# Expert rows: empty slots skipped by bounds, results scattered in token order

## The chip, the cores and the metric

The kernel runs on one core of a Trainium2 chip. The metric is the device time of one execution in microseconds (us).

## The reference, cut to what matters

The program is two transformer blocks. The second one has, in each of its two layers, a mixture of experts over T tokens of width D = 1024 (T = 512 in the first layer, 256 in the second): a router picks 2 of 32 experts per token, each expert is a gated feed-forward net of width 512, and a token's two results are added with their gates.

```python
def hier_moe(xf, ...):
    ...
    top_v, top_i = lax.top_k(e_in, TOP_K)
    gate = jax.nn.softmax(top_v, axis=-1) * g_val
    expert = g_idx * EXPERTS_PER_GROUP + top_i
    ...
    def expert_block(args):
        xblk, e = args
        return (jax.nn.silu(xblk @ w1[e]) * (xblk @ w3[e])) @ w2[e]
    yb = lax.map(expert_block, (xb, block_exp)).reshape(R, D)
    out = jnp.zeros((T + 1, D), yb.dtype).at[row_tok].add(yb * row_gate[:, None])
    return out[:T]
```

Everything is in float32. An expert's three matrices are 6.29 MB, so the 32 experts of a layer are 201 MB.

## The kernel before, in words

The stages run in order: four feed-forward nets with two mixers between them (first block), then `even`, `moe(0)`, `odd`, `moe(1)` (second block). Only `moe` and its router are touched by the change.

The router (VectorE, `moe` from line 1871) gives each of a token's two assignments a slot. A block is 64 slots (`BLK`) of one expert; block b belongs to expert b, and an expert's slots fill from the first. Extra blocks (16 and 8) exist for experts with more than 64 tokens; they are walked only if there are any. TensorE turns one-hot matrices into the table `token_of_slot` (line 918), where an empty slot gets token 0, and VectorE copies it out (line 1993). `slot_of_token` (line 1959) holds the slot of each assignment.

The expert loop handles one block per step, on all engines at once:

- SP (lines 550 to 582) loads the expert's weights in six pieces of 1 MB, four for w1 and w3 (named raw and work in the trace, both <-in_w) and two for w2, into six buffers. A load waits until TensorE has used the buffer (`expert_done`).
- GpSimd (`gather`, `rows_of`, lines 2172 to 2182) copies the block's column of the table, drains, and issues an indirect DMA that fetches all 64 rows of 4 KB from `router_rows` into `xg`, which has two buffers. It waits until TensorE has turned the rows that were in the buffer (`xgt_ready`), two blocks back.
- TensorE (`block_of`) does w1 and w3 for block b (lines 934, 936), turns the rows of b + 1 (line 927), does w2 for b - 1 (line 952) and turns the result of w1 and w3 (line 944).
- ACT copies the turned rows and the products, computes tanh, and stores the result of block b - 1 with two plain DMAs of 128 KB (line 1413) into `expert_rows`, ordered by slot.
- VectorE computes the activation and copies w2's result from PSUM to `ysb` (line 2015, `y_copied`), which has two buffers: it waits for the store two blocks back (`y_stored`).

After the loop GpSimd waits for all stores and gathers each token's two rows from `expert_rows` with indirect DMAs (line 2203), two per tile of 128 tokens: eight in the first layer, four in the second, 0.5 MB each. Before it waits for them, ACT in the first layer issues loads of the next layer's norm rows and makes the high halves of two weight panels (line 1128; VectorE's low halves are line 1537). It then scales the first row by its gate (line 1459), and VectorE adds the second row, multiplies, and adds to the residual (lines 2050 to 2054).

Once, early in the program (line 1316), ACT issues a 4 MB DMA that fills the rows of the extra blocks in `expert_rows`.

## Time and profile before

| | |
|---|---|
| median of 3 runs | 2908.72 us (2908.54 to 2909.84) |
| the profiled execution | 2905.86 us |
| its span, first to last instruction | 2904.0 us |
| TensorE busy (PE) | 2310.4 us, 80% |
| VectorE busy (DVE) | 1070.7 us, 37% |
| ScalarE busy (ACT) | 686.9 us, 24% |
| GpSimd busy (POOL) | 117.8 us, 4% |
| mean granted TensorE clock | 0.90 |
| data moved by DMA | 718.82 MB, mean 248 GB/s |

The profile is one execution. Its times count from the first instruction. PE is TensorE's matmuls, PEld its weight loads, SP the engine that issues the weight DMAs; a name that ends in q (SPq, ACTq, POOLq) is an engine's queue of instructions that issue or wait. The DMA share is the mean busy share of the core's 16 DMA engines; it can read a little over 1, where packets overlap. "Idle before" an instruction is the time its engine did nothing, with what ended it. The first expert stage runs from about 1484 to 2046 us, the second from about 2338 to 2892 us.

### The profile page before, as it was taken

To read this page: it belongs to the slowest core of one execution; us is meant where nothing else is said; L and a number is where in the kernel's file an instruction comes from. 1 tells how busy PE (TensorE), PEld (TensorE's weight loads), DVE (VectorE), ACT (ScalarE), POOL (GpSimd) and SP (SyncE) were. 2 spreads that over 40 slices of the span, in tenths; PEclk is the share of its full clock that TensorE was granted. 3 is DMA by queue.
4 is the path that set the end of the run, shared out by engine and by line. 5 is a ranking of instruction groups with operands and counts; after the bars stand their busy time and mean duration, and the time that the engine had idled before them with its cause. 6 is when DMAs were issued, how large, how long until landed. Compare 5 with 4: busy or idle time off the path is not lost.

```text
span 2904.0 us, 35200 instructions
## 1 busy us (share of the span) xinstructions
PE 2310.4 (80%) x13750; PEld 1590.7 (55%) x13750; DVE 1070.7 (37%) x1570; ACT 686.9 (24%) x876; POOL 117.8 (4%) x209
## 2 busy tenths in 40 slices
PE   5998679979987699699558777877369668888885
PEld 5888478878885688587523333332355523333332
DVE  4555545555556355723420100010668410000011
ACT  3334433333335233321101000100335200000100
POOL 0001000000010000000000000000100000000000
PEclk9999789989998799899669999999679788998898
DMA  7775137757752287422149999999420269999997
GB/s 260 261 238 173 56 118 266 253 190 266 262 169 88 104 288 259 139 78 94 73 161 401 399 396 400 402 400 404 179 71 1 87 258 397 401 399 401 401 402 303
DMA packets 242628, 718.82 MB, mean 248 GB/s; under 512 B 17040, under 2 KB 156560, under 8 KB 189072
## 3 DMA queue, kind: packets, MB, share of 16 engines
q1 hardware_dynamic: 213584, 642.82, 59.7%
q10 hardware_dynamic: 19952, 48.45, 4.6%
q0 software_dynamic: 8976, 25.90, 3.0%
q8 instruction: 87, 1.43, 0.2%
q14 instruction: 29, 0.24, 0.0%
HBM read 693.70 MB, written 25.26 MB: 248 GB/s over the span
## 4 chain that ended last, share of the span: by engine, by line
PE 55%; DMA 26%; DVE 9%; issue 4%; DVEq 2%; ACT 2%; SPq 1%; ACTq 0%; POOL 0%; POOLq 0%
DMA raw<-in_w 24%; PE ps L620 13%; PE ps L621 12%; PE ps L622 12%; PE ps L934 10%; PE ps L655 2%; PE ps L634 1%; SPq L554 1%; PE ps L936 1%; PE ps L1071 1%; DVE t_lo L1537 1%; PE ps L1086 1%; DMA raw<-in_ffn_w_up 1%; DVE work L1601 1%; DMA work<-expert_rows,slot_of_token 1%
## 5 line engine op out<-in xcount | busy, mean ns | idle before, releaser
L1537 DVE TENSOR_TENSOR w_lo<-raw,w_hi 128x2048 fp32r<-128x2048 f32 x180 | 411.4, 2290 | 445.1 <-ACT w_hi L1128 445.1
L620 PE MATMUL ps<-t_hi,w_hi 128*128 128x256 f32 (+1 forms) x1568 | 456.4, 291 | 8.7 <-DVE t_lo L1537 8.6
L621 PE MATMUL ps<-t_lo,w_hi 128*128 128x256 f32 (+1 forms) x1568 | 454.1, 290 | 0.0
L622 PE MATMUL ps<-t_hi,w_lo 128*128 128x256 f32 (+1 forms) x1568 | 451.1, 288 | 0.0
L1128 ACT CAST w_hi<-raw 128x2048 fp32r<-128x2048 f32 x180 | 342.1, 1903 | 447.5 <-PE ps L622 428.5
L934 PE MATMUL ps<-raw,work 128*64 128x512 f32 x528 | 308.8, 742 | 167.0 <-DMA raw<-in_w 165.6
L2015 DVE COPY work<-ps 128x512 f32<-128x512 f32 x64 | 44.3, 692 | 932.6 <-PE ps L952 932.6
L620 PE MATMUL ps<-w_hi,t_hi 128*128 128x256 f32 (+1 forms) x1088 | 349.8, 322 | 15.3 <-DVE t_lo L1537 12.4
L622 PE MATMUL ps<-w_hi,t_lo 128*128 128x256 f32 (+1 forms) x1088 | 351.1, 323 | 0.0
L621 PE MATMUL ps<-w_lo,t_hi 128*128 128x256 f32 (+1 forms) x1088 | 351.0, 323 | 0.0
L620 PEld LDWEIGHTS ps<-t_hi,w_hi 128*128 128x128 f32 x1568 | 296.6, 189 | 30.4 <-issue 13.2
L936 PE MATMUL ps<-raw,work 128*64 128x512 f32 x528 | 310.5, 745 | 0.0
L622 PEld LDWEIGHTS ps<-t_hi,w_lo 128*128 128x128 f32 x1568 | 297.6, 190 | 4.6
L621 PEld LDWEIGHTS ps<-t_lo,w_hi 128*128 128x128 f32 x1568 | 296.1, 189 | 5.6
L934 PEld LDWEIGHTS ps<-raw,work 128*64 128x64 f32 x528 | 82.7, 167 | 371.0 <-issue 369.2
L934 PE MATMUL ps<-work 128*64 128x512 f32 x496 | 228.9, 605 | 31.9 <-DMA work<-in_w 31.9
L936 PE MATMUL ps<-work 128*64 128x512 f32 x496 | 229.4, 606 | 0.0
L620 PEld LDWEIGHTS ps<-w_hi,t_hi 128*128 128x128 f32 x1088 | 211.2, 194 | 31.7 <-DVE t_lo L1537 13.5
L952 PE MATMUL ps<-raw,work 128*64 128x512 f32 x992 | 226.7, 598 | 0.2 <-DMA raw<-in_w 0.2
L622 PEld LDWEIGHTS ps<-w_hi,t_lo 128*128 128x128 f32 x1088 | 209.5, 193 | 14.1
L621 PEld LDWEIGHTS ps<-w_lo,t_hi 128*128 128x128 f32 x1088 | 209.3, 192 | 13.5
L1394 ACT COPY work<-ps 128x512 f32<-128x512 f32 x64 | 37.5, 586 | 712.2 <-PE ps L936 712.2
(280 smaller groups left out, 2159.1 us busy)
## 6 DMA issues: line engine op xcount, KB each, us to landing
raw<-in_w SPq DMA_DIRECT2D x256, 1024.0 KB, 11.3
work<-in_w SPq DMA_DIRECT2D x128, 1024.0 KB, 10.7
work<-in_w_mod SPq DMA_DIRECT2D x32, 1536.0 KB, 6.5
raw<-in_ffn_w_gate SPq DMA_DIRECT2D x44, 1024.0 KB, 8.8
raw<-in_ffn_w_up SPq DMA_DIRECT2D x44, 1024.0 KB, 10.3
raw<-in_ffn_w_down SPq DMA_DIRECT2D x44, 1024.0 KB, 4.9
raw<-in_w_in SPq DMA_DIRECT2D x18, 1024.0 KB, 5.5
expert_rows<-work ACTq DMA_DIRECT2D x128, 128.0 KB, 7.2
```

Of the source, the lines that this page charges most:

```text
L554: sp.dma_start(expert_raw(m, x).rearrange("p (a n) -> p a n", a=1), src).then_inc(expert_landed[x], 16)
L620: pe.matmul(dst, a[0], b[0], start=start, stop=False)
L621: pe.matmul(dst, a[0], b[1], start=False, stop=False)
L622: return pe.matmul(dst, a[1], b[0], start=False, stop=stop)
L655: mm = pe.matmul(ps[32 * q:32 * q + 32, bank + a // BANK, 0:n], cond[:, kk, :], mod_raw[:, q * MOD_Q + a:q * MOD_Q + a + n], start=True, s ...
L934: first = pe.matmul(ps[0:BLK, 2 + par, :], xT[:, par, kk * BLK:(kk + 1) * BLK], w1[:, j * BANK:(j + 1) * BANK], start=kk == 0, stop=kk == ...
L936: mm = pe.matmul(ps[BLK:P, 2 + par, :], xT[:, par, kk * BLK:(kk + 1) * BLK], w3[:, j * BANK:(j + 1) * BANK], start=kk == 0, stop=kk == KD - 1)
L952: mm = pe.matmul(ps[BLK * half:BLK * half + BLK, 6 + par, :], am[:, par, c * BLK:(c + 1) * BLK], w2[:, j * D + half * BANK:j * D + (half + ...
L1128: act.copy(slot(j)[0], src).then_inc(w_hi_ready, 1)
L1394: act.copy(gusb[:, par, :], ps[:, 2 + par, :]).then_inc(gu_ready, 1)
L1537: return dve.tensor_tensor(dst, src, hi.bitcast(F32), ALU.subtract)
L2015: dve.tensor_copy(ysb[:, par, :], ps[:, 6 + par, :]).then_inc(y_copied, 1)
```

## The change

Three things. The table's entries now hold an assignment instead of a token: 4 * token + 2 * k + half for the row in the result, and that number shifted right by two for the token; an empty slot gets a number beyond every valid one. The gather and the new scatter name a bound, and rows beyond it are skipped. The result goes to `expert_rows` in token order by an indirect DMA from GpSimd (128 rows of 2 KB, two per slot, valid ones only), in place of ACT's two plain stores; a token's two results then lie side by side, and ACT loads them with one plain 1 MB DMA per tile of 128 tokens.

GpSimd's order in the loop is: gather of block b + 4, scatter of block b. The gather waits as before; the scatter waits for VectorE's copy of block b and for the landing of the scatter before it. ACT, after its loop, waits for all scatters, issues the loads, and only then the loads of norm rows and the two weight splits. The fill of the extra rows is dropped. TensorE makes the table for both halves (twice the small matmuls), and the count of extra blocks gets a place per layer.

```diff
-    put("tokid", i[:, None] + P * np.arange(4)[None, :])
+    put("tokid", 2 * (i[:, None] + P * (np.arange(8) % 4)[None, :]) + (np.arange(8) // 4)[None, :] - 4096)
+    put("halfid", 8192 + (i >= BLK))
...
-    y_dram = nc.dram_tensor("expert_rows", (BLOCKS[0] * BLK, D), F32, kind="Internal").ap()
+    y_dram = nc.dram_tensor("expert_rows", (4 * P * 4, BANK), F32, kind="Internal").ap()
...
                 for i in range(2 * nt):
-                    mm = pe.matmul(ps[0:BLK, 2, 0:nb], r_onehot[:, i, :], r_blk[:, i, 0:nb], start=i == 0, stop=i == 2 * nt - 1)
+                    for half in range(2):
+                        mm = pe.matmul(ps[BLK * half:BLK * half + BLK, 2, 0:nb], r_onehot[:, i, :], r_blk[:, i, 0:nb],
+                                       start=i == 0, stop=i == 2 * nt - 1)
...
-                if l == 1:
-                    act.dma_start(y_dram[EXPERTS * BLK:, :], A["w_out"][0][0:EXTRA[0] * BLK, :]).then_inc(extra_filled, 16)
...
-                def store(b, par):
-                    act.wait_ge(y_copied, b0 + b + 1)
-                    for dst, src in out_rows(b * BLK, par):
-                        act.dma_start(dst, src).then_inc(y_stored[par], 16)
...
+                act.wait_ge(expert_done, MAIN * (m + 1))
+                for par in range(2):
+                    act.wait_ge(y_stored[par], 8 * (b0 + EXPERTS))
+                for t in range(nt):
+                    act.dma_start(yg[t].rearrange("p c n -> p (c n)"),
+                                  y_dram.rearrange("(r c) n -> r (c n)", c=4)[t * P:(t + 1) * P, :]).then_inc(yg_landed[t], 16)
                 if m == 0:
-                    act.wait_ge(expert_done, MAIN)
                     act.wait_ge(mod_stored, 64 * 4)
                     norm_rows(10)
                     split(G0["odd"])
                     split(G0["odd"] + 1)
                 for t in range(nt):
-                    act.wait_ge(yg_landed[t], 32 * (m + 1))
+                    act.wait_ge(yg_landed[t], 16 * (m + 1))
...
-                    dve.tensor_copy(slot_id[:, 0:nt, kk], r_sl[:, kk, 0:nt])
...
-                dve.tensor_copy(table[0:BLK, 0:nb], ps[0:BLK, 2, 0:nb])
+                dve.tensor_scalar(rows_table[:, 0:nb], ps[:, 2, 0:nb], 2.0, k("halfid"), ALU.mult, ALU.add)
+                dve.drain()
+                dve.tensor_scalar(table[0:BLK, 0:nb], rows_table[0:BLK, 0:nb], 2, None, ALU.logical_shift_right)
                 dve.drain().then_inc(table_ready, 1)
...
-                        dve.wait_ge(y_stored[par], 16 * (b0 + b - par))
+                        dve.wait_ge(y_stored[par], 8 * (b0 + b - par))
...
-                def rows_of(b, par):
+                def rows_in(b, par):
 
                     pool.tensor_copy(table_col[0:BLK, par:par + 1], table[0:BLK, bass.ds(b, 1)])
                     pool.drain()
                     return pool.indirect_dma_start(out=xg[0:BLK, par, :], out_offset=None, in_=h_dram,
-                                                   in_offset=bass.IndirectOffsetOnAxis(ap=table_col[0:BLK, par:par + 1], axis=0))
+                                                   in_offset=bass.IndirectOffsetOnAxis(ap=table_col[0:BLK, par:par + 1], axis=0),
+                                                   bounds_check=nt * P - 1, oob_is_err=False)
+
+                def rows_out(b, par):
+
+                    pool.tensor_copy(rows_col[:, par:par + 1], rows_table[:, bass.ds(b, 1)])
+                    pool.drain()
+                    return pool.indirect_dma_start(out=y_dram, in_=ysb[:, par, :], in_offset=None,
+                                                   out_offset=bass.IndirectOffsetOnAxis(ap=rows_col[:, par:par + 1], axis=0),
+                                                   bounds_check=4 * nt * P - 1, oob_is_err=False)
...
+                def scatter(b, par, first=False):
+                    pool.wait_ge(y_copied, b0 + b + 1)
+                    if not first:
+                        pool.wait_ge(y_stored[1 - par], 8 * (b0 + b + par))
+                    rows_out(b, par).then_inc(y_stored[par], 16)
...
-                with pool.Fori(1, EXPERTS // 2) as i:
+                gather(2, 0)
+                gather(3, 1)
+                gather(4, 0)
+                scatter(0, 0, first=m == 0)
+                gather(5, 1)
+                scatter(1, 1)
+                with pool.Fori(3, EXPERTS // 2) as i:
                     gather(2 * i, 0)
+                    scatter(2 * i - 4, 0)
                     gather(2 * i + 1, 1)
+                    scatter(2 * i - 3, 1)
+                for b in range(EXPERTS - 4, EXPERTS):
+                    scatter(b, b % 2)
...
-                for par in range(2):
-                    pool.wait_ge(y_stored[par], 16 * (b0 + EXPERTS))
-                for t in range(nt):
-                    for kk in range(2):
-                        pool.indirect_dma_start(out=yg[t][:, kk, :], out_offset=None, in_=y_dram,
-                                                in_offset=bass.IndirectOffsetOnAxis(ap=slot_id[:, t, kk:kk + 1], axis=0)
-                                                ).then_inc(yg_landed[t], 16)
```

## Rows read from the trace of the kernel before

**Rows 1.** Stretches: length, each engine's busy us (instructions), granted clock, DMA share, GB/s

```profile
1850.00:2000.00 150.00, 116.27 (x538) 46.00 (x537) 13.81 (x27) 14.00 (x27) 8.71 (x16) 0.97 1.02 403
...
2500.00:2700.00 200.00, 167.16 (x714) 63.50 (x710) 18.42 (x36) 18.67 (x36) 13.12 (x24) 0.91 1.01 401
```

**Rows 2.** DMA queues and issues, 2400 to 2740 us, with us to landing

```profile
q1 hardware_dynamic: 17211, 125.32, 92.2%
q0 software_dynamic: 1600, 5.24, 5.2%
q10 hardware_dynamic: 3200, 5.25, 4.1%
...
expert_rows<-work ACTq DMA_DIRECT2D x40, 128.0 KB, 7.6
work<-router_rows,token_of_slot_col POOLq DMA_INDIRECT x20, 7.7
```

**Rows 3.** The chain that ended last: start us, us, what

```profile
1560.66 12.93 DMA raw<-in_w
...
1987.40 11.14 DMA raw<-in_w
...
2502.52 10.74 DMA raw<-in_w
2519.39 10.91 DMA raw<-in_w
...
2825.49 10.82 DMA raw<-in_w
```

**Rows 4.** Waits, 2400 to 2840 us, the TensorE line: us, times, longest

```profile
PE ps L934 <- DMA raw<-in_w: 73.2, 26, 3.6
```

**Rows 5.** Busy time by stretch inside two blocks, columns as rows 1

```profile
2502.00:2508.00 6.00, 6.00 (x34) 2.72 (x35) 1.10 (x2) 1.47 (x3) 1.10 (x2) 1.00 1.01 418
2508.00:2511.00 3.00, 2.73 (x14) 0.70 (x10) 0.44 (x2) 0.00 (x0) 0.00 (x0) 1.00 1.02 325
...
2512.00:2519.00 7.00, 5.60 (x19) 2.09 (x20) 0.00 (x0) 0.21 (x1) 0.00 (x0) 0.76 1.02 425
...
2525.00:2528.00 3.00, 2.62 (x14) 0.59 (x10) 0.40 (x1) 0.00 (x0) 0.00 (x0) 1.00 1.04 306
```

**Rows 6.** GpSimd in order of time: start us, us, what, idle before

```profile
2337.93 0.93 POOL L2176 DMA_INDIRECT work<-router_rows,token_of_slot_col  x1 [1.43 <-issue]
2338.86 0.19 POOL L2174 COPY token_of_slot_col<-token_of_slot 64x1 uint32<-64x1 uint32 x1
2342.26 0.92 POOL L2176 DMA_INDIRECT work<-router_rows,token_of_slot_col  x1 [3.20 <-issue]
...
2504.07 0.92 POOL L2176 DMA_INDIRECT work<-router_rows,token_of_slot_col  x1 [0.84 <-issue]
```

**Rows 7.** The chain at the first gather of the second stage

```profile
2337.93 3.55 DMA work<-router_rows,token_of_slot_col
```

**Rows 8.** The final gathers, line 2203: what each took, and DMA to landing

```profile
L2203 POOL DMA_INDIRECT work<-expert_rows,slot_of_token x12: 937/940/2062, 2034.9 to 2888.7; - x12
...
DMA to landing us min/median/max: 4.3/9.3/10.9
```

**Rows 9.** The chain at the end of each expert stage

```profile
2028.30 5.81 DMA expert_rows<-work
...
2036.18 9.96 DMA work<-expert_rows,slot_of_token
...
2881.84 2.38 DMA expert_rows<-work
...
2886.24 5.50 DMA work<-expert_rows,slot_of_token
```

**Rows 10.** The slot tables in order of time, TensorE and VectorE

```profile
1473.21 1.94 PE L918 MATMUL ps<-work 128*64 128x48 f32 x16 [11.44 <-DVEq L1976]
...
1477.05 0.18 DVE L1993 CAST token_of_slot<-ps 64x48 uint32<-64x48 f32 x1
```

More of the change, by code:

```diff
@@ L165, in build @@
         table_col = sb("token_of_slot_col", [P, 2], U32)
+        rows_table = sb("row_of_slot", [P, BLOCKS[0]], U32)
+        rows_col = sb("row_of_slot_col", [P, 2], U32)
         extra_id = sb("extra_expert", [P, EXTRA[0]], I32)
@@ L1403, in tanh, with block_of @@
                                    scale=0.5).then_inc(mtanh_ready, 1)
-                def out_rows(row0, par):
-                    return [(y_dram[bass.ds(row0, BLK), half * BANK:(half + 1) * BANK], ysb[BLK * half:BLK * half + BLK, par, :])
-                            for half in range(2)]
-                def store(b, par):
-                    act.wait_ge(y_copied, b0 + b + 1)
-                    for dst, src in out_rows(b * BLK, par):
-                        act.dma_start(dst, src).then_inc(y_stored[par], 16)
-                def block_of(b, par, last=False, stored=True):
+                def block_of(b, par, last=False):
                     up_copy(b, par)
@@ L1419, in block_of @@
                     tanh(b, par)
-                    if stored:
-                        store(b - 1, 1 - par)
                 rows_T(0, 0)
-                block_of(0, 0, stored=False)
+                block_of(0, 0)
                 block_of(1, 1)
@@ L1430, in moe @@
                 block_of(EXPERTS - 1, 1, last=True)
-                store(EXPERTS - 1, 1)
-                act.wait_ge(extra_filled, 16)
-                used = act.value_load(extra_used[0:1, 0:1], min_val=0, max_val=EXTRA[m])
+                used = act.value_load(extra_used[0:1, m:m + 1], min_val=0, max_val=EXTRA[m])
                 with act.If(used > 0):
@@ L1443, in moe @@
                                        scale=0.5).then_inc(ex_tanh[m], 1)
-                        act.wait_ge(ex_y[m], i + 1)
-                        for dst, src in out_rows((i + EXPERTS) * BLK, 0):
-                            act.dma_start(dst, src).then_inc(ex_stored[m], 16)
+                    act.wait_ge(ex_stored[m], 16 * EXTRA[m])
                     act.drain()
@@ L2028, in moe @@
                 out_rows(EXPERTS - 1, 1, MAIN)
-                used = dve.value_load(extra_used[0:1, 0:1], min_val=0, max_val=EXTRA[m])
+                used = dve.value_load(extra_used[0:1, m:m + 1], min_val=0, max_val=EXTRA[m])
                 with dve.If(used > 0):
-                    dve.wait_ge(y_stored[0], 16 * (b0 + EXPERTS))
+                    dve.wait_ge(y_stored[0], 8 * (b0 + EXPERTS))
                     with dve.Fori(0, EXTRA[m]) as i:
@@ L2037, in moe @@
                         dve.tensor_copy(ysb[:, 0, :], ps[:, 6, :]).then_inc(ex_y[m], 1)
-                        dve.wait_ge(ex_stored[m], 32 * i + 32)
+                        dve.wait_ge(ex_stored[m], 16 * i + 16)
                     dve.drain()
@@ L2181, in gather @@
                         pool.wait_ge(xgt_ready, b0 + b - 1)
-                    rows_of(b, par).then_inc(xg_landed[m][par], 16)
+                    rows_in(b, par).then_inc(xg_landed[m][par], 16)
+                def scatter(b, par, first=False):
[3 more added lines that the diff above has]
+                    rows_out(b, par).then_inc(y_stored[par], 16)
                 gather(0, 0, True)
                 gather(1, 1, True)
-                with pool.Fori(1, EXPERTS // 2) as i:
+                gather(2, 0)
[5 more added lines that the diff above has]
+                with pool.Fori(3, EXPERTS // 2) as i:
                     gather(2 * i, 0)
+                    scatter(2 * i - 4, 0)
                     gather(2 * i + 1, 1)
-                used = pool.value_load(extra_used[0:1, 0:1], min_val=0, max_val=EXTRA[m])
+                    scatter(2 * i - 3, 1)
+                for b in range(EXPERTS - 4, EXPERTS):
+                    scatter(b, b % 2)
+                used = pool.value_load(extra_used[0:1, m:m + 1], min_val=0, max_val=EXTRA[m])
                 with pool.If(used > 0):
                     pool.wait_ge(xgt_ready, b0 + EXPERTS)
+                    for par in range(2):
+                        pool.wait_ge(y_stored[par], 8 * (b0 + EXPERTS))
                     with pool.Fori(0, EXTRA[m]) as i:
-                        rows_of(i + EXPERTS, 0).then_inc(ex_gathered[m], 16)
-                        pool.wait_ge(ex_stored[m], 32 * i + 32)
+                        rows_in(i + EXPERTS, 0).then_inc(ex_gathered[m], 16)
+                        pool.wait_ge(ex_y[m], i + 1)
+                        rows_out(i + EXPERTS, 0).then_inc(ex_stored[m], 16)
+                        pool.wait_ge(ex_stored[m], 16 * i + 16)
                     pool.drain()
```

10 lines of the change are left out of this document (4 added, 6 removed).

## The prediction

> **What bounds the kernel now.** I went from the whole to the part: the busy time by stretch, the DMA queues, the chain of waits, the waits of the engines, and last the stretches inside one block and GpSimd in order of time. Both expert stages run at a DMA share of 1.01 to 1.02 and about 400 GB/s while TensorE is busy 78% and 84% of the time [rows 1]: the reader is to see that the DMA engines, not TensorE, have no room. The queues say what they carry: of 20 blocks' traffic 125.32 MB is weights, 5.24 MB gathered rows, 5.25 MB stored rows [rows 2]. The chain repeats one pattern per expert block: a 10.8 us weight load, TensorE, the next load. Its first and last starts give the period: (1987.40 - 1560.66) / 25 = 17.07 us in the first stage and (2825.49 - 2502.52) / 19 = 17.00 us in the second [rows 3]. Bytes give the same: 6 loads of 1.049 MB are 6.29 MB, gather and store are 0.262 MB each (64 rows of 4 KB), together 6.82 MB, at 401 GB/s 17.0 us. TensorE waits 73.2 us for weights in 26 blocks, 2.8 us per block [rows 4], so a block can shrink to about 14.2 us before TensorE sets its length.
>
> Inside a block the rate is not even. It is 418 to 425 GB/s for most of it, but 325 and 306 GB/s in the 3 us that begin 4 us after a gather is issued [rows 5, 6], at a full DMA share. The gather costs more than its bytes: it drags the weights that move beside it. The stores fall in the stretch at 425 GB/s and do not.
>
> **The parts, priced.** A block has 64 slots, but the two experts of 512 (256) tokens fill only 1024 (512) of the 2048 slots that 32 blocks have. So on average 32 of 64 rows are real in the first stage and 16 of 64 in the second. Before, all 64 are moved.
>
> Gather, price of a full one. From above: its bytes at 425 GB/s, 0.62 us, and the rate lost beside it, 3 x (425 - 325) / 425 = 0.70 us or 3 x (425 - 306) / 425 = 0.84 us [rows 5]; 1.4 us. From below: bytes alone at 401 GB/s, 0.65 us.
>
> Store, price of a full one: 0.62 to 0.65 us by its bytes. The new scatter goes through GpSimd's queue, which the trace has only as gathers, so its price is open: as cheap per byte as a store, or as dear as a gather (1.4 us when full).
>
> First stage, half the rows. Most: 0.70 (gather) + 0.31 (scatter priced as a store) = 1.01 us saved. Least: 0.33 + 0.31 = 0.64 by bytes alone; a dear scatter with a dear gather gives 0.70 - 0.08 = 0.62. Second stage, a quarter. Most: 1.05 + 0.47 = 1.52 us. Least: 0.49 + 0.49 = 0.98 by bytes. I take 0.75 and 1.15 us, nearer to the least, since that needs no more than that bytes not moved take no time, and skipped rows may leave something behind. Over 31 periods each (the first block overlaps the router): 23 + 36 = 59 us; ends 50 and 78 us. The new periods, 16.3 and 15.85 us, stay above TensorE's 14.2 us, so nothing else is late next.
>
> A rule bears on what draws the rate down. The Trainium skill, SBUF — State Buffer, section "SBUF: two separate sides", says DMA reaches SBUF through AXI ports with a swizzled partition map, where DMA engines can contend. By it a gather into 64 partitions crowds half the ports, and a scatter read from all 128 is cheap; the trace agrees as far as 325 GB/s in the gather and 425 in the store go, and by this rule the sum would lie at the upper end, 78 us.
>
> ACT loses two store issues per block and gains four loads per stage: nothing, it waits for TensorE anyway. SP's queue is not touched.
>
> GpSimd gets the scatter, and here queueing matters. An indirect DMA that follows another goes out only after the first has landed: the copy for the second gather is done at 2339.05, yet its DMA goes at 2342.26, 0.8 us after the first one's landing at 2341.48 (2337.93 + 3.55) [rows 6, 7]; with nothing outstanding the gap is 0.84 us. I read that as the drain between copy and DMA. So gather, 0.8 us, scatter, 0.8 us, next gather run in series, and the wait for the previous scatter costs nothing more. A full gather lands in 7.7 us under load, a store in 7.6 us [rows 2]; full size, the series is 16.9 us, just what a block has. With fewer rows the part in which packets move (3 us) halves or quarters: 6.2 + 6.1 + 1.6 = 13.9 us in the first stage, 5.5 + 5.4 + 1.6 = 12.5 us in the second, against 16.3 and 15.85. It stays hidden by 2 to 3 us. Gathers are issued two blocks before TensorE turns them, as before, so latency alone does no harm.
>
> Tables: 16 (8) more small matmuls cost up to 1.9 us, of which some 1.7 us lie beside VectorE's work that ends with the table at 1477.05 [rows 10]; VectorE's extra instruction and drain about 0.3 us, two casts fewer give 0.15 back. Cost 0.3 us per stage. The 4 MB fill of the table's tail goes; nothing waited for it: 0.
>
> Tails. Last rows: the store's landing (5.81 and 2.38 us) [rows 9] gives way to copy, drain, scatter: about 1 us before it and a gather's idle-queue landing of 3.55 us [rows 7], so 2 us later. In its place four (two) plain 1 MB loads from ACT replace pairs of gathers that took 9.96 and 5.50 us to land after their second issue [rows 9], about 2 us better, as GpSimd's 1.0 us start and the 0.5 MB pieces go. Together 0, bounds 3 us either way per stage. In the first stage the last scatter also waits for the one before it, and ACT's two weight splits now stand behind its wait for the scatters; both lie beside the landing. If that cover is gone they cost up to the 3 us.
>
> Sum: -59 + 0.6 + 0 = -58 us. The profiled execution took 2905.86 us (span 2904.0), which gives 2848; the median of the runs is 2.9 us above it, so 2851 us.
>
> **Rivals.**
> (a) Uneven shedding. Real rows fill the first slots. If each DMA engine serves fixed rows, those with the first rows shed little, and a 1 MB load lands when its slowest share does. If the busiest keeps its whole gather share and half its scatter share, a block saves 0.31 us plus part of the 0.7 to 0.84 us of drag: 0.3 to 0.9 us per block in both stages, 19 to 56 us; I take 35: 2874 us. For: nothing in the rows is per engine. Against: the full drag was seen with all 64 rows. The Trainium skill, DMA: Bandwidth & Descriptors, "The descriptor swizzle", gives engine 0 partitions 0 to 3 and 32 to 35 of a 128-partition transfer. No row here shows it; by it the second stage saves half of its scatter rather than three quarters.
> (b) All drag goes with the rows, and the scatter is as cheap as a store: the upper ends, -78 us, 2831 us. For: 425 GB/s beside stores. Against: the kept rows still sit in the first partitions. It is the case that the port rule above gives.
> (c) GpSimd becomes the bound, and the kernel slower. Its place is the drain between gather and scatter. It decides where the two landings plus 1.6 us exceed 17.0 us, so from 15.4 us in landings. If skipping does not shorten them and a scatter of 128 half rows takes the 9.3 us of the 128-row final gathers [rows 8], a block is 7.7 + 9.3 + 1.6 = 18.6 us: +1.6 x 62 = +99 us, 3008 us. With the gather shortened, 6.2 + 9.3 + 1.6 = 17.1: no gain in the first stage. For: 9.3 us. Against: that was eight 0.5 MB gathers queued behind each other; the scatter has 0.26 MB at most.
> (d) The skipped rows are still moved, or replaced by packets as costly: the same bytes, 2905 to 2912 us. Against: the diff bounds both sides below the value of an empty slot.
>
> **Chances.** Forecast 0.60, (a) 0.18, (b) 0.12, (c) 0.07 (of this 0.05 slower, the rest a small gain), (d) 0.03. The range runs from just beyond (b), 2826, to 2888, which takes in most of (a). About 0.2% (6 us) is what a measurement of this kernel can tell from no change. Faster 0.92, same 0.03, slower 0.05.
>
> **What would show it.** Period between the repeating weight loads in the chain: 16.3 and 15.85 us; still a DMA share of 1.0 and 400 GB/s or more; the software queue's bytes in the loop falling to half and a quarter for gathers; the dip to 325 GB/s shorter; TensorE's wait per block 2.1 and 1.7 us. Scatter issues some 0.8 us after the gather's landing show the drain. Wrong if the periods stay at 17 us, if the GpSimd series fills the period (its copies no longer waiting for TensorE), or if DMA share falls under 0.95.

## The result and the profile after

The changed kernel takes 2845.04 us (median of 4 runs, 2844.16 to 2845.29), the kernel before 2908.63 us beside it: ratio 0.978, 95% interval 0.9763 to 0.9797. That is 63.6 us faster; 2851 us was forecast, range 2826 to 2888. The profiled execution took 2844.16 us, 61.7 us less than the one before.

From the page of the changed kernel, the span, TensorE, GpSimd in 40 slices, and the DMA queues (packets, MB, share of the 16 engines):

```profile
span 2842.3 us, 35337 instructions
...
PE 2276.9 (80%) x13774; PEld 1586.7 (56%) x13774; DVE 1071.1 (38%) x1568; ACT 686.8 (24%) x876; POOL 185.1 (7%) x325
...
POOL 0001000000001000000001111111000001111110
...
q1 hardware_dynamic: 213584, 642.82, 60.6%
q10 hardware_dynamic: 10496, 33.76, 3.3%
q0 software_dynamic: 12368, 15.45, 1.8%
```

ACT's queue lost its 128 stores and the fill (48.45 MB before, 33.76 now), the software queue moves 15.45 MB where it moved 25.90, and GpSimd has work all through both expert stages. SP's queue moves the same 642.82 MB. The two expert stages, columns as in [rows 1]:

```profile
1700.00:1850.00 150.00, 122.94 (x556) 48.22 (x556) 13.82 (x27) 14.00 (x27) 22.22 (x37) 0.95 1.01 405
2500.00:2700.00 200.00, 162.15 (x750) 64.54 (x748) 19.96 (x39) 19.06 (x37) 29.46 (x50) 0.97 1.01 407
```

The DMA share is 1.01 as before: the bound has not moved. The chain of waits, first and last weight load of the steady part of each stage, answers to [rows 3]:

```profile
1558.13 11.57 DMA raw<-in_w
...
1915.91 11.60 DMA raw<-in_w
...
2387.17 9.62 DMA raw<-in_w
...
2751.89 9.65 DMA raw<-in_w
```

(1915.91 - 1558.13) / 22 = 16.26 us and (2751.89 - 2387.17) / 23 = 15.86 us per block, against 17.07 and 17.00. Over the whole of each loop, from the first to the last of VectorE's 32 copies of w2's result, the kernel before takes 515.3 and 514.8 us, the changed one 491.3 and 478.9: 24.0 + 35.9 = 59.9 us less (0.77 and 1.16 us in each of 31 blocks), nearly all of the gain. The DMA queues and issues from 2400 to 2740 us (answers to [rows 2]; the last column is us from issue to landing):

```profile
q1 hardware_dynamic: 18567, 135.20, 97.7%
q0 software_dynamic: 3440, 3.10, 2.9%
...
work<-router_rows,token_of_slot_col POOLq DMA_INDIRECT x22, 6.8
expert_rows<-work,row_of_slot_col POOLq DMA_INDIRECT x21, 6.5
```

About 22 blocks now move 3.10 MB through the software queue, 0.14 MB per block where gather and store moved 0.52. That is a quarter, so the skipped rows' bytes are gone. Their packets are not: the whole execution has 12368 packets in this queue, exactly as many as e3 below, which moves every row by the same two DMAs, and e1, which only bounds the gather, has the 8976 of the kernel before. A skipped row leaves a packet of a few bytes behind. (That there are more than before, 12368 against 8976, comes from the results, which now go through this queue.) The small packets take hardly any time: 2.9% for 3.10 MB is 0.94% per MB, and in e3 the same stretch has 9.1% for 10.49 MB, 0.87% per MB.

Three waits, 2400 to 2780 us (us, times, longest), answer to [rows 4]:

```profile
POOL token_of_slot_col L2165 <- PE ps L930: 136.7, 24, 7.9
...
PE ps L937 <- DMA raw<-in_w: 45.7, 24, 2.2
...
PE ps L937 <- DMA work<-in_w: 22.9, 18, 1.4
```

TensorE waits (45.7 + 22.9) / 24 = 2.9 us per block, as before, although the block is 1.1 us shorter. The busy time makes up for it: 162.15 us in 200 us of 15.86 us blocks is 12.9 us per block, against 167.16 us in 17.0 us blocks, 14.2 us [rows 1], and the granted clock is 0.97 where it was 0.91. TensorE spent less of each block at the lower of its two levels. GpSimd still waits for TensorE, 136.7 / 24 = 5.7 us per block.

Inside one block (columns as in [rows 1]; the gather is issued at 2531.76, the scatter at 2539.84), answers to [rows 5]:

```profile
2530.00:2532.00 2.00, 2.00 (x13) 1.00 (x14) 0.00 (x0) 0.70 (x2) 0.41 (x2) 1.00 0.88 299
...
2535.00:2538.00 3.00, 3.00 (x16) 0.86 (x12) 0.84 (x2) 0.19 (x1) 0.18 (x1) 1.00 1.02 362
2538.00:2540.00 2.00, 0.36 (x2) 0.00 (x0) 0.00 (x0) 0.00 (x0) 0.16 (x1) 1.00 1.02 422
...
2544.00:2546.00 2.00, 2.00 (x14) 1.32 (x16) 0.00 (x0) 1.17 (x2) 0.18 (x1) 1.00 1.04 424
```

The stretch in which the gather moves (2535 to 2538) runs at 362 GB/s. One block says little, so here is the mean rate in the 3 us that begin 4 us after a gather's issue, over the 20 to 22 gathers from 1560 to 1900 us and from 2400 to 2740 us: 305 and 307 GB/s before, 350 and 381 now. The drag got less, but by less than the rows did: half of the rows leave 0.53 us of it where there was 0.85 (3 x (425 - 350) / 425 against 3 x (425 - 305) / 425), a quarter leaves 0.31 us. The stretch in which the scatter moves (2544 to 2546) is at 424: no drag.

From 2530 to 2532 the share is 0.88 and the rate 299 GB/s. Here SP's next four loads have just gone out (2529.62). It is not this block alone: over the 3 us from each such issue the mean is 393 and 396 GB/s in the two stages, with a share down to 0.86, where the kernel before has 420 and 417. In such a stretch some of the DMA engines are idle; e4 and e11 below bear on why.

### The profile page after: what moved, and what is told of

The parts are those of the page before. It is cut to its first block, busy times and chain, and to the rows that moved or that the text cites. A ratio compares the mean times of both kernels' runs of the same rounds, so it can differ in the third digit from the quotient of the medians.

```text
span 2842.3 us, 35337 instructions
## 1 busy us (share of the span) xinstructions
PE 2276.9 (80%) x13774; PEld 1586.7 (56%) x13774; DVE 1071.1 (38%) x1568; ACT 686.8 (24%) x876; POOL 185.1 (7%) x325
## 3 DMA queue, kind: packets, MB, share of 16 engines
q1 hardware_dynamic: 213584, 642.82, 60.6%
q10 hardware_dynamic: 10496, 33.76, 3.3%
q0 software_dynamic: 12368, 15.45, 1.8%
## 4 chain that ended last, share of the span: by engine, by line
PE 55%; DMA 25%; DVE 9%; issue 6%; DVEq 2%; ACT 2%; SPq 1%; ACTq 0%; POOLq 0%
DMA raw<-in_w 21%; PE ps L621 13%; PE ps L622 13%; PE ps L623 13%; PE ps L937 9%; DMA expert_rows<-work,row_of_slot_col 2%; PE ps L656 2%; PE ps L635 1%; SPq L555 1%; PE ps L1074 1%; PE ps L1089 1%; PE ps L939 1%; DMA raw<-in_ffn_w_up 1%; DVE t_lo L1527 1%; DVE work L1591 1%
## 5 line engine op out<-in xcount | busy, mean ns | idle before, releaser
L937 PE MATMUL ps<-raw,work 128*64 128x512 f32 x528 | 275.7, 672 | 121.0 <-DMA raw<-in_w 119.6
L939 PE MATMUL ps<-raw,work 128*64 128x512 f32 x528 | 277.4, 676 | 0.0
L937 PE MATMUL ps<-work 128*64 128x512 f32 x496 | 224.9, 596 | 53.8 <-DMA work<-in_w 53.7
L937 PEld LDWEIGHTS ps<-raw,work 128*64 128x64 f32 x528 | 75.5, 153 | 303.8 <-issue 302.0
L955 PE MATMUL ps<-raw,work 128*64 128x512 f32 x992 | 226.5, 598 | 0.0
L939 PE MATMUL ps<-work 128*64 128x512 f32 x496 | 226.1, 598 | 0.0
L635 PE MATMUL ps<-consts,work 128*128 128x128 f32 x208 | 42.1, 391 | 198.3 <-DVE work L1591 119.9
```

Of the source, the lines that this page charges most:

```text
L635: mm = pe.transpose(ps[:, j, q * P:(q + 1) * P], hrow[:, t, kk * P:(kk + 1) * P], ident)
L937: first = pe.matmul(ps[0:BLK, 2 + par, :], xT[:, par, kk * BLK:(kk + 1) * BLK], w1[:, j * BANK:(j + 1) * BANK], start=kk == 0, stop=kk == ...
L939: mm = pe.matmul(ps[BLK:P, 2 + par, :], xT[:, par, kk * BLK:(kk + 1) * BLK], w3[:, j * BANK:(j + 1) * BANK], start=kk == 0, stop=kk == KD - 1)
L955: mm = pe.matmul(ps[BLK * half:BLK * half + BLK, 6 + par, :], am[:, par, c * BLK:(c + 1) * BLK], w2[:, j * D + half * BANK:j * D + (half + ...
```

## The experiments

The periods below are worked out from the first and the last of VectorE's copies of w2's result (line 2015 before, 2006 after) in 1550 to 1900 us and in 2400 to 2750 us of each trace, 19 to 22 blocks. They are good to 0.1 or 0.2 us only, since in the changed kernel blocks of 14.3, 16 and 18 us follow each other and a window can hold one more of the long ones. So the two last columns give the whole loop of each stage, from the first to the last of the 32 copies, 31 blocks; the changed kernel and its repeat e12 differ there by 0.8 us, 0.03 us per block. What a block costs is taken from them.

| kernel | time, us | ratio to before (95%) | period 1, us | period 2, us | loop 1, us | loop 2, us |
|---|---|---|---|---|---|---|
| before | 2908.63 | | 16.97 | 17.06 | 515.3 | 514.8 |
| changed | 2845.04 | 0.978 (0.9763 to 0.9797) | 16.36 | 15.86 | 491.3 | 478.9 |
| e1 bound on the gather alone | 2858.09 | 0.9825 (0.9806 to 0.9844) | 16.39 | 16.10 | 495.5 | 488.2 |
| e2 scatter skips, gather full | 2892.29 | 0.9943 (0.9924 to 0.9962) | 17.02 | 16.74 | 509.2 | 507.3 |
| e3 nothing skipped | 2909.1 | 0.9998 (0.9986 to 1.001) | 17.04 | 17.14 | 515.7 | 516.6 |
| e4 rows spread | 2837.43 | 0.9755 (0.9735 to 0.9775) | 16.17 | 15.72 | 489.1 | 473.7 |
| e5 splits first | 2842.96 | 0.9781 (0.9765 to 0.9797) | 16.36 | 15.95 | 490.7 | 479.7 |
| e6 scatter first | 2843.32 | 0.9777 (0.9764 to 0.979) | 16.31 | 15.85 | 491.5 | 478.8 |
| e7 wide gather | 2867.01 | 0.9852 (0.9826 to 0.9878) | 16.20 | 16.76 | 490.3 | 511.1 |
| e8 one drain | 2841.81 | 0.9765 (0.9752 to 0.9778) | 16.38 | 15.88 | 490.5 | 479.1 |
| e9 spread, one drain | 2834.32 | 0.9741 (0.9728 to 0.9755) | 16.21 | 15.73 | 490.0 | 473.7 |
| e10 distinct rows | 2909.95 | 0.9996 (0.9987 to 1.0005) | 17.20 | 17.04 | 516.5 | 514.9 |
| e11 rows packed | 2888.7 | 0.9928 (0.9911 to 0.9944) | 16.88 | 16.89 | 508.9 | 504.5 |
| e12 changed again | 2843.11 | 0.9769 (0.9753 to 0.9785) | 16.36 | 15.91 | 490.5 | 479.7 |

### One half of the change at a time: e1, e2, e3

e1, on the kernel before:

```diff
-    put("tokid", i[:, None] + P * np.arange(4)[None, :])
+    put("tokid", i[:, None] + P * np.arange(4)[None, :] - 2048)
...
-                dve.tensor_copy(table[0:BLK, 0:nb], ps[0:BLK, 2, 0:nb])
+                dve.tensor_scalar(table[0:BLK, 0:nb], ps[0:BLK, 2, 0:nb], 2048.0, None, ALU.add)
...
+                                                   bounds_check=nt * P - 1, oob_is_err=False)
```

> The kernel before, with the bound on the gather alone: empty slots get a token number beyond the bound; ACT still stores all 64 rows in slot order. Theory (bytes and the drag beside them): a gather costs 1.4 us when full, so 0.70 and 1.05 us per block go, 31 blocks each, 54 us in all: about 2855 us. Rival (bytes alone): 0.33 and 0.49 us per block, 25 us: about 2883 us. Rival (busiest DMA engine keeps its rows): under 15 us gained, 2894 us or more.

2858.09 us, 51.7 us less than before in the same rounds: near the theory with the drag, not bytes alone. The loops lost 0.64 and 0.86 us per block, 46.4 us together. In the trace, the rate in the 3 us that begin 4 us after a gather's issue rose from 305 and 307 GB/s to 358 and 379.

e2, on the changed kernel:

```diff
-                dve.tensor_scalar(table[0:BLK, 0:nb], rows_table[0:BLK, 0:nb], 2, None, ALU.logical_shift_right)
+                dve.tensor_scalar(table[0:BLK, 0:nb], rows_table[0:BLK, 0:nb], 2, 511, ALU.logical_shift_right, ALU.bitwise_and)
```

> The changed kernel with the gather unbounded again (an empty slot fetches token 0); the scatter still skips. Theory (drag): the 54 us come back, about 2899 us. Rival (bytes alone): 25 us, about 2870 us. The GpSimd series is 7.7 + 6.5 + 1.8 = 16.0 us, still under the period of 16.7 us or more, so it adds nothing.

2892.29 us, 47 us more than the changed kernel. The loops give 0.58 and 0.92 us per block for the skipped gather rows, where e1 gives 0.64 and 0.86.

e3 is e2 with room for 8192 more rows in `expert_rows`, a row of its own for each empty slot, and the scatter's bound beyond them:

```diff
+                spare = r_ex[:, 0:2, :].rearrange("p a b -> p (a b)")[:, 0:nb]
+                dve.tensor_scalar(spare, ps[:, 2, 0:nb], 0.0, k("rowid"), ALU.is_equal, ALU.mult)
...
-                                                   bounds_check=4 * nt * P - 1, oob_is_err=False)
+                                                   bounds_check=8192 + P, oob_is_err=False)
```

> The changed kernel with every row moved: the gather fetches token 0 for empty slots, the scatter writes empty slots to spare rows of their own behind the real ones. If the scatter costs what the stores did per byte: the time before, 2905 to 2915 us. If it is as dear as a gather: 0.78 us more in 62 blocks, about 2957 us. If the GpSimd series is the bound, with 7.7 us for the gather and up to 9.3 us for the scatter: a period of up to 18.8 us, 3020 us, and GpSimd's copies no longer wait for TensorE.

2909.1 us: the time before. Moving the result by GpSimd's scatter in token order, with everything moved, costs and brings nothing; a full scatter costs what two plain stores cost. All of the gain is in the rows that are skipped. By the loops, from e3 to e2 the scatter's skipping alone gives 0.21 and 0.30 us per block; from e1 to the changed kernel it gives 0.13 and 0.30 us. Its bytes would give 0.31 and 0.47 us. (The periods of the windows alone would say 0.02 to 0.03 us for the first stage and 0.24 to 0.40 for the second. For the first stage that is an accident of which blocks they hold.) e4 and e11 say where a part of the difference goes.

### Where the drag comes from: e7, e10

e7, on the kernel before: the same 0.262 MB gathered to 128 partitions of 2 KB.

```diff
-                    pool.tensor_copy(table_col[0:BLK, par:par + 1], table[0:BLK, bass.ds(b, 1)])
+                dve.tensor_copy(table[BLK:P, 0:nb], k("tokid")[BLK:P, 0:1].to_broadcast([BLK, nb]))
...
+                    pool.tensor_copy(table_col[:, par:par + 1], table[:, bass.ds(b, 1)])
...
-                    return pool.indirect_dma_start(out=xg[0:BLK, par, :], out_offset=None, in_=h_dram,
-                                                   in_offset=bass.IndirectOffsetOnAxis(ap=table_col[0:BLK, par:par + 1], axis=0))
+                    return pool.indirect_dma_start(out=xg[:, par, 0:BANK], out_offset=None, in_=h_dram.rearrange("r (c n) -> (r c) n", c=2),
+                                                   in_offset=bass.IndirectOffsetOnAxis(ap=table_col[:, par:par + 1], axis=0))
```

> The kernel before, with the full gather's 0.262 MB brought to 128 partitions of 2 KB in place of 64 partitions of 4 KB. The experts work on wrong rows: the upper half of the packets and the second half of each row of the block are left out of the computation's sense; all instructions and bytes stay. If the drag (325 GB/s beside the gather) comes from a gather that reaches only 64 partitions: it goes, 0.70 to 0.84 us in 62 blocks, 2857 to 2866 us. If it comes from the software queue or from the source rows: 2905 us or more, since there are twice as many packets.

The upper 64 partitions read half-rows 64 to 127 of `router_rows`, whatever the router said.

2867.01 us, 41 us less, with the same bytes. GpSimd's issue of one gather, and two stretches of 3 us from 4 us after it:

```profile
2526.32 0.96 POOL L2177 DMA_INDIRECT work<-router_rows,token_of_slot_col  x1 [0.83 <-issue]
```

```profile
2530.00:2533.00 3.00, 2.98 (x14) 0.72 (x10) 0.69 (x2) 0.00 (x0) 0.00 (x0) 1.00 1.00 369
2533.00:2536.00 3.00, 0.61 (x4) 0.38 (x6) 0.00 (x0) 0.00 (x0) 0.00 (x0) 1.00 1.00 404
```

369 GB/s, where the gather to 64 partitions ran at 306 and 325 [rows 5]. The two stages differ. In the first the drag is all but gone in every block (mean 415 GB/s over 21 gathers, none under 401), the loop is 25.0 us shorter, 0.81 us per block, as the drag was priced, and the gather's packets take 4.0% of the engines' time for 4.72 MB (1600 to 1900 us) where they took 5.3%, with the same 1440 packets. In the second the mean is 370 GB/s, the single gathers lie between 314 and 415, and the loop is only 3.7 us shorter. The profiled execution is one of the two longer ones of four (2873.14 us; the others took 2859.65, 2860.88 and 2877.16), so the second stage may well gain more in the others; no trace shows it, and why the drag comes back there was not found. The median stands 1 us beyond the range expected. e7 also changed which rows are read: its upper half always reads the same 64 half-rows, while in the kernel before every empty slot reads row 0. So e10 was needed: 64 partitions and rows of 4 KB as before, but an empty slot p reads row p.

```diff
+                dve.tensor_scalar(spare, ps[0:BLK, 2, 0:nb], 0.0, k("rowid")[0:BLK, :], ALU.is_equal, ALU.mult)
+                dve.drain()
+                dve.scalar_tensor_tensor(table[0:BLK, 0:nb], ps[0:BLK, 2, 0:nb], 2048.0, spare, ALU.add, ALU.add)
```

> The kernel before, where an empty slot of the gather fetches the row with the slot's own number in place of row 0; 64 partitions, 64 rows of 4 KB as before, and the same result. It is the control for the wide gather, which changed the source rows too. If the drag comes from 64 partitions alone: 2905 us or more, no change. If it comes from the many reads of one row: it goes, 40 us or more, 2870 us or less.

2909.95 us, ratio 0.9996, and 301 and 307 GB/s in the 3 us: reading one row 32 to 48 times is not what costs. The drag comes with the 64 partitions of 4 KB: with 128 of 2 KB it is gone in the first stage, and in the second only in part. Number and bytes of the packets are the same in both forms (80 packets per gather). Whether the number of partitions matters or the length of a row was not separated.

### Does it matter which rows stay: e4, e11

e4, on the changed kernel, spreads an expert's rows over its block:

```diff
                     dve.tensor_copy(r_sli[:, kk, 0:nt], r_sl[:, kk, 0:nt])
+                    dve.tensor_scalar(r_ini[:, kk, 0:nt], r_sl[:, kk, 0:nt], 5.0, None, ALU.mult)
...
-                    dve.tensor_scalar(r_ini[:, kk, 0:nt], r_sli[:, kk, 0:nt], BLK - 1, None, ALU.bitwise_and)
+                    dve.tensor_scalar(r_ini[:, kk, 0:nt], r_ini[:, kk, 0:nt], BLK - 1, None, ALU.bitwise_and)
```

> The changed kernel with an expert's rows spread over the 64 slots of its block (slot number times 5, modulo 64) in place of the first ones. Theory (the kept rows load the DMA engines evenly enough, the bound is the sum of bytes): 2842 to 2848 us. Rival (uneven shedding: the busiest engine or port keeps more than its share): 0.1 to 0.5 us per block are to be had, 6 to 31 us: 2814 to 2839 us.

2837.43 us, 7.6 us below the changed kernel and 5.7 us below its repeat e12; the intervals of the ratios overlap, but both loops are shorter, by 1.4 to 2.2 us in the first stage and by 5.2 to 6.0 in the second (against e12 and against the changed kernel). e11 does the opposite: slots 0 to 3, 32 to 35, 4 to 7, 36 to 39 and so on.

```diff
+                    dve.tensor_scalar(r_ini[:, kk, 0:nt], r_sli[:, kk, 0:nt], 3, None, ALU.bitwise_and)
+                    dve.tensor_scalar(packed[:, kk, 0:nt], r_sli[:, kk, 0:nt], 4, 3, ALU.bitwise_and, ALU.logical_shift_left)
+                    dve.tensor_scalar(packed[:, kk, 4:4 + nt], r_sli[:, kk, 0:nt], 1, 28, ALU.logical_shift_right, ALU.bitwise_and)
...
+                    dve.tensor_tensor(r_inf[:, kk, 0:nt], r_ini[:, kk, 0:nt], packed[:, kk, 0:nt], ALU.add)
...
+                    dve.tensor_tensor(r_inf[:, kk, 0:nt], r_inf[:, kk, 0:nt], packed[:, kk, 4:4 + nt], ALU.add)
```

> The changed kernel with an expert's rows packed into as few groups of partitions as can be: slots 0 to 3, 32 to 35, 4 to 7, 36 to 39 and so on, the opposite of the spread. Same rows, same bytes. Theory of uneven shedding: the first groups keep all 8 of their rows, as in a full gather, and the time goes back toward the 2892 us of the full gather: 2852 to 2890 us. Theory that only the sum counts: 2842 to 2848 us (the extra 0.1 us of VectorE per layer is nothing).

2888.7 us, beside 2843.11 us for the changed kernel in the same rounds. It moves the same rows and bytes, and 45.6 us of the gain of 67.5 us are lost. Little of the time is lost beside the gather: the mean rate in the 3 us that begin 4 us after its issue is 340 and 384 GB/s in the two stages, where the changed kernel has 350 and 381. (Single gathers vary; the stretch from 2494 to 2497 us, after the gather issued at 2489.96, is at 337.) It is lost where SP's next four loads go out. One such issue is at 2555.43 here and one at 2554.05 in e4, both near the means below; e11 first, then e4 (columns as in [rows 1]):

```profile
2555.00:2558.00 3.00, 3.00 (x18) 1.59 (x18) 0.00 (x0) 1.17 (x2) 0.61 (x2) 1.00 0.89 306
```

```profile
2554.00:2557.00 3.00, 3.00 (x18) 1.57 (x20) 0.00 (x0) 1.12 (x2) 0.19 (x2) 1.00 1.04 429
```

The mean rate and the lowest share of the DMA engines in the 3 us from each such issue, over 19 to 22 blocks of each stage (1560 to 1900 and 2400 to 2740 us):

| kernel | GB/s, stage 1 | GB/s, stage 2 | lowest share |
|---|---|---|---|
| before | 420 | 417 | 0.99 |
| e4 rows spread | 421 | 418 | 0.98 |
| changed | 393 | 396 | 0.86 |
| e12 changed again | 393 | 390 | 0.87 |
| e11 rows packed | 344 | 308 | 0.75 |

Among the kernels that skip, the order of the rates is the order of the times. With full blocks or spread rows the engines stay busy up to the next loads; with the rows in few groups some of them idle. The reading that fits is that the engines with few rows run out of work while the busiest still holds up the weight loads that TensorE waits for; the profile has no row for a single engine, so it is not shown engine by engine. Either way the time depends on which partitions the rows lie in, not on their sum alone. Gather and scatter both take part: the same stretch of the second stage has 402 GB/s when only the gather skips (e1) and 413 when only the scatter does (e2). By e4's loops spreading gives back 0.04 to 0.07 us per block in the first stage and 0.17 to 0.19 in the second. The dip beside the gather is no better when the rows are spread (341 and 376 GB/s).

The Trainium skill, DMA: Bandwidth & Descriptors, "The descriptor swizzle", names just these groups (partitions 0 to 3 with 32 to 35, and so on) as served by one DMA engine, in a transfer over 128 partitions. Slots 0 to 3 and 32 to 35 come first in e11 for that reason, and the runs agree with the rule (2888.7 us packed by it, 2843.11 us with the first slots in a row). Whether the busiest engine or its port into SBUF holds things up, these runs can't tell.

e12 is the changed kernel itself, run again beside e11.

> The changed kernel itself, on the same chip and in the same rounds as the packed one, for a comparison without the spread between chips. 2840 to 2848 us.

2843.11 us, ratio 0.9769 (0.9753 to 0.9785).

### GpSimd's series: e6, e8, and the two together with the spread, e9

GpSimd in the changed kernel, in order of time (start, us, what, idle before), answers to [rows 6]:

```profile
2530.68 0.18 POOL L2165 COPY token_of_slot_col<-token_of_slot 64x1 uint32 x1 [7.59 <-PE ps L930]
2531.76 0.97 POOL L2167 DMA_INDIRECT work<-router_rows,token_of_slot_col  x1 [0.90 <-issue]
2535.19 0.18 POOL L2173 COPY row_of_slot_col<-row_of_slot 128x1 uint32 x1 [2.46 <-DVE work L2006]
2539.84 1.03 POOL L2175 DMA_INDIRECT expert_rows<-work,row_of_slot_col  x1 [4.46 <-issue]
2545.15 0.18 POOL L2165 COPY token_of_slot_col<-token_of_slot 64x1 uint32 x1 [4.28 <-PE ps L930]
2547.12 0.97 POOL L2167 DMA_INDIRECT work<-router_rows,token_of_slot_col  x1 [1.79 <-issue]
```

The gather goes at 2531.76, the scatter's copy is done at 2535.37, and the scatter goes at 2539.84: 8.1 us after the gather, whose landing takes 6.8 us at the median. The next gather is 0.9 us behind its copy when the scatter has landed by then, and 1.79 us where it has not (2547.12). So the series was 6.8 + 6.5 + 1.8 = 15.1 us of a period of 15.86.

e6 turns the order around in the loop:

```diff
-                    gather(2 * i, 0)
                     scatter(2 * i - 4, 0)
-                    gather(2 * i + 1, 1)
+                    gather(2 * i, 0)
                     scatter(2 * i - 3, 1)
+                    gather(2 * i + 1, 1)
```

> The changed kernel with the order on GpSimd turned around: scatter of block b, then gather of block b + 4. Theory (a gather has two blocks of slack): no change, 2842 to 2848 us. Rival (the order carries part of the gain: the gather now stands behind the wait for VectorE's copy and the landing of the scatter): TensorE waits for rows, 2855 us or more.

2843.32 us, no change. Each gather now goes 7.4 us after the scatter:

```profile
2531.04 1.02 POOL L2175 DMA_INDIRECT expert_rows<-work,row_of_slot_col  x1 [0.93 <-issue]
2532.06 0.20 POOL L2165 COPY token_of_slot_col<-token_of_slot 64x1 uint32 x1
2538.40 0.96 POOL L2167 DMA_INDIRECT work<-router_rows,token_of_slot_col  x1 [6.14 <-issue]
```

and nothing waits for it.

e8 makes the copy of the scatter's column ahead of the gather, with the gather's own; the last four scatters read their column from the table itself. (The small copy from `consts` only carries the wait.)

```diff
+                def both(b, par, first=False):
+                    pool.tensor_copy(rows_col[:, par:par + 1], rows_table[:, bass.ds(b - 4, 1)])
+                    pool.wait_ge(xgt_ready, b0 + b - 1)
+                    rows_in(b, par).then_inc(xg_landed[m][par], 16)
+                    pool.wait_ge(y_copied, b0 + b - 4 + 1)
...
+                    pool.tensor_copy(rows_col[0:1, 2:3], iota[0:1, bass.ds(b, 1)])
+                    out_of(rows_col[:, par:par + 1], par).then_inc(y_stored[par], 16)
```

> The changed kernel with GpSimd's copy of the scatter's column made ahead of the gather, so that no drain stands between the gather and the scatter of a block; the last four scatters take their column from the table itself, with no copy and no drain. Theory (the drain holds the scatter until the gather has landed, and the series is hidden): the scatter goes 1 us or less after VectorE's copy in place of 4.5 us after it, the period stays at 16.3 and 15.9 us, and each tail gets shorter by the copy and the drain, 1.1 us: about 2843 us. Rival (the series is part of the bound): the period falls by 0.1 us or more per block, 2838 us or less. Rival (the gap is the making of descriptors, not the drain): the scatter still goes 4 us after the copy.

```profile
2530.09 0.96 POOL L2167 DMA_INDIRECT work<-router_rows,token_of_slot_col  x1 [1.00 <-issue]
2533.43 0.18 POOL L2196 CAST row_of_slot_col<-consts 1x1 uint32 x1 [2.38 <-DVE work L2006]
2534.20 1.03 POOL L2172 DMA_INDIRECT expert_rows<-work,row_of_slot_col  x1 [0.59 <-issue]
```

The scatter goes at 2534.20, 0.8 us after VectorE's copy has released it and 4.1 us after the gather's issue, so before the gather can have landed. The drain was the gate. The loops, 490.5 and 479.1 us, did not move: the series was hidden. From VectorE's last copy to the first sum it is 19.2 and 9.95 us in place of 19.9 and 10.4, so 1.2 us come from the tails where 2.2 were expected; 2841.81 us can't be told from the changed kernel's time.

e9 is the edits of e4 and of e8 together.

> The spread rows and the single drain together. If the two add up: 8 us from the spread and 2 us from the tails, about 2835 us.

2834.32 us, the fastest kernel of this study: 10.7 us below the changed kernel, 10 expected, and 8.8 below its repeat e12. Nearly all of it is the spread's.

### The first tail: e5

The changed kernel's first tail in order of time: VectorE's last copy, the last scatter, the four loads, VectorE's splits, the first sum.

```profile
2003.67 0.69 DVE L2006 COPY work<-ps 128x512 f32<-128x512 f32 x1 [3.76 <-PE ps L955]
...
2006.79 0.99 POOL L2175 DMA_INDIRECT expert_rows<-work,row_of_slot_col  x1 [0.90 <-issue]
2012.46 2.07 ACTq L1439 DMA_DIRECT2D work<-expert_rows  x4
...
2019.16 4.49 DVE L1527 TENSOR_TENSOR w_lo<-raw,w_hi 128x2048 fp32r<-128x2048 f32 x2 [14.80 <-ACT w_hi L1131]
...
2023.57 1.28 DVE L2041 SCALAR_TENSOR_TENSOR work<-work,gates 128x1024 f32<-128x1024 f32 x1
```

e5 moves ACT's loads of norm rows and its splits back ahead of the wait for the scatters:

```diff
+                if m == 0:
+                    act.wait_ge(mod_stored, 64 * 4)
+                    norm_rows(10)
+                    split(G0["odd"])
+                    split(G0["odd"] + 1)
                 for par in range(2):
                     act.wait_ge(y_stored[par], 8 * (b0 + EXPERTS))
...
-                if m == 0:
-                    act.wait_ge(mod_stored, 64 * 4)
-                    norm_rows(10)
-                    split(G0["odd"])
-                    split(G0["odd"] + 1)
```

> The changed kernel with ACT's loads of norm rows and its two weight splits again ahead of its wait for the scatters and of the loads of the expert rows. In the changed kernel's first tail VectorE's half of the splits ends at 2023.6 us and the sum of the expert rows starts right there. Theory (the splits are the cover that ends last): the sum starts about 4 us earlier, 2841 us. Rival (the norm rows' 2.5 MB go ahead of the expert rows on ACT's queue and delay them): 2844 us or more.

```profile
2001.65 0.69 DVE L2006 COPY work<-ps 128x512 f32<-128x512 f32 x1 [3.76 <-PE ps L955]
...
2005.95 4.50 DVE L1527 TENSOR_TENSOR w_lo<-raw,w_hi 128x2048 fp32r<-128x2048 f32 x2 [3.61 <-ACT w_hi L1131]
2011.70 1.77 ACTq L1444 DMA_DIRECT2D work<-expert_rows  x4
...
2020.85 1.28 DVE L2041 SCALAR_TENSOR_TENSOR work<-work,gates 128x1024 f32<-128x1024 f32 x1 [10.40 <-ACT work L1449]
```

The splits end 10 us before the first sum, and still it starts 19.2 us after VectorE's last copy (2001.65 to 2020.85), where it was 19.9 us (2003.67 to 2023.57). The loads, issued at 2011.70, land later: the norm rows ahead of them on ACT's queue took the cover's place. That is the rival's mechanism, with 0.7 us gained where 4 were expected; 2842.96 us against 2845.04 can't be told from no change.

## Why the prediction was right

**The bound** held: DMA share 1.01, chain of weight loads, periods 16.26 and 15.86 us where 16.3 and 15.85 were forecast.

**Gather.** Its full price of 1.4 us (bytes 0.62, drag 0.70 to 0.84) gave 0.70 and 1.05 us per block if the drag fell with the rows; e1 and e2 measured 0.58 to 0.64 and 0.86 to 0.92. The mechanism was right, but the drag fell more slowly than the rows: from 0.85 us to 0.53 and 0.31. With the bytes (0.31 and 0.47) that makes 0.63 and 1.01 us. The total that the prediction took was near bytes alone; for the gather the true value was nearer to the upper end.

**Scatter.** Between "as cheap as a store" (0.31 and 0.47 us saved) and "as dear as a gather" (-0.08 and 0.27), the runs gave 0.13 to 0.21 and 0.30. Whole it costs what stores cost (e3), and no drag stands beside it. It saves less than its bytes. The sum had no term for kept rows that lie in few groups of partitions, and the spread of e4 gives back 0.04 to 0.07 and 0.17 to 0.19 us per block; the rest stays open.

So the gather saved more than bytes alone and the scatter less. The two errors cancel, 0.75 and 1.15 us taken, 0.77 and 1.16 found. That the periods were met this closely is luck: the terms behind them were not met.

**Rival (a), uneven shedding,** was given 0.18 as the whole story. It is real and part of the story: with rows in the first slots it costs 6 to 8 us (e4), packed as badly as can be 45.6 us (e11), and the engines' share falls where SP's next loads go out. It took too much away: it had a block save 0.3 to 0.9 us in both stages, and 0.77 and 1.16 were found. Rows in slots 0 to 31 fill no group of eight by more than half. The 32 rows of the first stage (on average) fill all eight groups alike, and spreading them gained 1.4 to 2.2 us; the 16 rows of the second fill only four groups, and there it gained 5 to 6 us.

**Rival (b), everything goes.** The drag beside the gather stayed in part (350 and 381 GB/s), and the scatter, whole as cheap as the stores (e3), saved less than its bytes. Its time, 2831 us, was come near only with the spread (e9, 2834.32 us).

**GpSimd.** The drain's wait was read rightly [rows 6, 7] and shown by e8. The landings were mis-sized: 7.1 and 6.6 us in the first stage, not 6.2 and 6.1, and 6.8 and 6.5 us in the second, not 5.5 and 5.4; only the part in which packets move got shorter, and by less than in proportion. The margin in the second stage was 0.8 us, not the 2 to 3 us claimed. Rival (c) was nearer than its chance of 0.07 said.

**TensorE's wait** was forecast at 2.1 and 1.7 us per block and stayed at 2.9: its busy time per block fell from 14.2 to 12.9 us with the granted clock at 0.97. The floor of 14.2 us was no floor, since it was counted at the clock of before.

**Tables and tails.** The first gather goes 0.90 us later than before (1484.60 against 1483.70), of which 0.65 us was there ahead of the router (the store of the rows lands at 1440.55, not 1439.90). That leaves 0.25 us for the tables, 0.3 forecast. The first tail took 19.9 us from VectorE's last copy to the first sum against 20.3 (2027.07 to 2047.41); the splits, not the landing, ended last, a cover the prediction had named as free. In the second tail the last scatter, the load and the first sum are in the chain as

```profile
2817.06 2.32 DMA expert_rows<-work,row_of_slot_col
...
2822.73 2.34 DMA expert_rows<-work,row_of_slot_col
...
2825.17 4.86 DMA work<-expert_rows
...
2831.32 1.28 DVE work L2041
```

From the last copy at 2820.89 to the first sum it is 10.4 us against 12.4: 2 us gained, 0 forecast. The scatter landed in 2.3 us on idle queues, not in a gather's 3.55, and the load in 4.86. All together: 24.0 and 35.95 us from the loops, 0.44 and 1.97 from the tails are 62.35 us gained. The first loop begins 0.59 us later than before, and 0.06 us is lost between the first tail and the second loop. That leaves the 61.7 us between the two profiled executions.

## What to carry to other kernels

Price a DMA by the rate of its neighbours too: a transfer that touches only part of the partitions can cost more than twice its bytes when the queues are full, and the fine stretches of the profile show it before any change is made. Take such a rate over many blocks, not from one. When rows are skipped, look at which remain: with the rows in few groups of partitions some DMA engines were idle while the load queue was the bound, and spreading the rows cost two small VectorE instructions per layer. On GpSimd, a drain between two indirect DMAs waits for the first to land; make the second one's indices ahead of it.

## What the runs showed that was not expected

- Same rows and bytes, packed into few groups of partitions: 2888.7 us against 2843.11 us (e11).
- In the packed kernel (e11) the share of the DMA engines falls as low as 0.75 in the 3 us from SP's issue of its next loads; with the rows spread (e4) it stays at 0.98 or more.
- A scatter with half its rows skipped saved 0.13 to 0.21 us per block, with three quarters skipped 0.30 us; its bytes would give 0.31 and 0.47.
- Skipped rows leave their packets behind: 12368 packets in the software queue with and without skipping (changed and e3), at 15.45 MB against 36.39.
- The same 0.262 MB to 128 partitions in place of 64 took 41 us off the kernel before (e7), in the profiled execution 25.0 us in the loop of the first stage and 3.7 in that of the second, while the choice of source rows did nothing (e10).
- In the second stage's shorter blocks the granted clock of TensorE was 0.97, where it was 0.91 before. Why it rose was not tested.
